# Gates of the last sixteen expert steps applied before the activations are stored

## The chip, the cores and the metric

The kernel runs on one core of a Trainium2 chip. The metric is the time of one execution on the device, in microseconds (us); lower is better. It is compared as the median of several executions. One execution is also recorded by the hardware profiler; its rows are used below.

## What is computed

One decoder layer for 544 tokens (512 of a prompt, 32 being sampled). An input projection feeds block-sparse attention and a convolution module, an output projection adds their results to the residual, and then comes the part that this change touches, a mixer of 128 x 128 = 16384 single-neuron experts, of which each of eight heads picks sixteen per token:

```python
idx = jnp.take_along_axis(cidx, pos, axis=-1)
g = jax.nn.softmax(top, axis=-1).astype(xc.dtype)
act = jax.nn.gelu(jnp.einsum('nd,nhkd->nhk', xc, expert_u[idx]), approximate=False)
return jnp.einsum('nhk,nhkd->nd', g * act, expert_v[idx])
```

## The kernel before

The kernel doesn't gather experts for most tokens. It computes all 16384 activations for all tokens as a dense product (the **up phase**), multiplies them with a matrix of gates that is zero where an expert wasn't picked, and multiplies the result with all of V (the **down phase**). Only the first 128 tokens (P) get their down product by gathered rows; the other 416 (ND) go through the dense one.

Both phases have 64 steps of 256 experts. To keep float32 accuracy on TensorE, each operand is split in a rounded part and a rest (`_hi`, `_lo`), and each product is three matmuls (lines 1394 to 1396).

**Up step s.** SP loads 1 MB of u into one of two buffers w_raw. ScalarE rounds it to w_hi (high_u, line 798), GpSimd makes w_lo (line 552), TensorE does 96 matmuls of 272 columns in two halves j. Behind each half ScalarE writes GELU to act_out (line 816), and SP stores act_out to the scratch tensor acts in HBM (line 411). SP's order within a step: wait for w_lo of step s + 1, load u of step s + 2, wait for both GELUs of step s, store them.

**Gates.** During steps 32 to 44 the matrix of gates is made and stored in HBM. It is loaded back by quads of four steps: 1664 KB for each of 16 quads into one of two halves of g_in (load_gates, line 427).

**Down step c.** SP loads act (416 KB, columns of the 416 tokens, line 424) into one of two buffers, and V in four parts to a quad, part k into v_raw[k]: w_raw[0], w_raw[1], v_raw_2 (which lies over act_out) and v_raw_3. DVE multiplies act with the gates (gate_acts, line 1325, two products of 128x416), ScalarE rounds it to a_hi (high_a, line 871), DVE makes a_lo (low_acts, line 1333). ScalarE rounds V to w_hi (high_v, line 864) once the down step two before is done, DVE makes w_lo (split_v, line 1338). TensorE then does 48 matmuls of 416 columns, and DVE adds two blocks to the residual (line 1313). DVE also adds up the 128 gathered rows (line 1355), GpSimd fetches them and the activations that belong to them (lines 568 and 561).

Every engine works through its own list in order. DVE's list for a down step is: second block of c - 1, gate_acts(c + 4), split_v(c + 1), some rows, first block of c, low_acts(c + 4), more rows.

TensorE's step c waits for `v_lo_done` of c and, at the first part of a quad, for `a_done` of all four steps of the quad.

**Between the phases.** After step 45 SP loads the gates of quads 0 and 1 and acts of steps 0 and 1; acts 2 and 3 follow after steps 48 and 49. DVE and ScalarE prepare down steps 0 to 3 in the middle of the up phase: ScalarE calls high_a(0, k) after the steps in PREPARE_AFTER (47, 48, 50, 51). At the end of the up phase SP stores the last acts, loads V parts 3 and 2 of quad 0, then acts of steps 4 and 5, then the gates of quad 2.

Of the kernel before, what the change touches and what calls it, by code (L numbers as in the profile page):

```python
# [8 lines left out]
ALU = mybir.AluOpType  # L9
# [3 lines left out]
P = 128  # L13
# [5 lines left out]
N = SEQ + NDEC  # L19
# [28 lines left out]
STEPS = 64  # L48
GCHUNK = 32
# [8 lines left out]
AFTER_GATES = RANK_STEPS + NG  # L58
PREPARE_AFTER = tuple(AFTER_GATES + n for n in (2, 3, 5, 6))
SCORE_BANKS = (4, 5, 6, 7)  # L60
# [34 lines left out]
def build_layer(nc, io):  # L95
# [95 lines left out]
    act_out = sb("act_out", [P, 2, 2, N])  # L191
# [80 lines left out]
    acts_loaded = [sem("acts_loaded0"), sem("acts_loaded1")]  # L272
    gated, a_high = sem("gated"), sem("a_high")
    g_made, g_kept = sem("g_made"), sem("g_kept")
# [75 lines left out]
    with nc.Block() as block:  # L350

        @block.sync
        def _(sp):
# [55 lines left out]
            def store_acts(s, slot):  # L409
                sp.wait_ge(gelu_done, 2 * s + 2)  # L410
                sp.dma_start(acts[s], act_out[:, slot, :, :].rearrange("p j n -> p (j n)"))\
                    .then_inc(acts_stored[slot], 16)
# [33 lines left out]
            for half in range(2):  # L446
                load_gates(half, half)
                sp.wait_ge(acts_stored[half], 32)
                load_acts(half, half)
            for s in range(AFTER_GATES + 1, AFTER_GATES + 7):  # L450
                up_step(s, s % 2)
                if AFTER_GATES + 3 <= s <= AFTER_GATES + 4:
                    first = s - AFTER_GATES - 3
                    sp.wait_ge(a_done, 2 * first + 2)
                    load_acts(first + 2, first)
            with sp.Fori((AFTER_GATES + 7) // 2, STEPS // 2 - 1) as i:
                up_step(2 * i, 0)
                up_step(2 * i + 1, 1)
            for slot in range(2):
                sp.wait_ge(u_lo_done, STEPS - 1 + slot)  # L460
                load_v(0, slot)
                store_acts(STEPS - 2 + slot, slot)
            load_v(0, 3)
# [21 lines left out]

            with sp.Fori(0, STEPS // 8 - 2) as it:
                for k in range(8):
                    down_step(it, k)
            it = STEPS // 8 - 2
            for k in range(8):  # L490
                c = 8 * it + k
                sp.wait_ge(v_lo_done, c + 1)
                load_v(2 * it + k // 4 + 1, k % 4)
                sp.wait_ge(a_done, 2 * c + 10)
                load_acts(c + 6, k % 2)
                if k == 3:
                    sp.wait_ge(gated, 2 * c + 10)
                    load_gates(2 * it + 3, 1)
            for k in range(4):
                down_step(STEPS // 8 - 1, k, True)  # L500
            sp.wait_ge(rows_added, 1)
# [85 lines left out]
        def _(sc):  # L587
# [278 lines left out]
            def high_a(it, k):  # L866

                s, slot = 8 * it + k, k % 2
                for j in range(2):
                    sc.wait_ge(gated, 2 * s + j + 1)  # L870
                    sc.activation(a_hi[k // 4 % 2][:, 2 * (k % 4) + j, :], act[:, slot, j, :], ACT.Copy)\
                        .then_inc(a_high, 1)

            plain_step(AFTER_GATES, 1, 16 * (AFTER_GATES // 2), 16 * (AFTER_GATES // 2 + 2))
            for s in range(AFTER_GATES + 1, AFTER_GATES + 7):
                plain_step(s, s % 2, 16 * (s // 2), 16 * ((s + 1) // 2) + 16)
                if s in PREPARE_AFTER:
                    high_a(0, PREPARE_AFTER.index(s))
            with sc.Fori((AFTER_GATES + 7) // 2, STEPS // 2 - 1) as i:
                plain_step(2 * i, 0, 16 * i, 16 * i + 16)  # L880
                plain_step(2 * i + 1, 1, 16 * i, 16 * i + 32)
            plain_step(STEPS - 2, 0, 8 * STEPS - 16, 8 * STEPS)
            sc.wait_ge(up_done, 2 * STEPS - 2)
            high_v(0, 64)
            for j in range(2):
                gelu_out(STEPS - 1, 1, j, 8 * STEPS - 16)
            sc.wait_ge(up_done, 2 * STEPS)
            high_v(1, 64)
# [9 lines left out]

            with sc.Fori(0, STEPS // 8 - 1) as it:
                for k in range(8):  # L900
                    down_step(it, k)
# [7 lines left out]
        def _(v):  # L909
# [406 lines left out]
            def gate_acts(s):  # L1316

                slot = s % 2
                v.wait_ge(acts_loaded[slot], 16 * (s // 2) + 16)
                if s % 4 == 0:  # L1320
                    v.wait_ge(g_loaded[s // 4 % 2], 16 * (s // 8) + 16)
                for j in range(2):
                    tile = 2 * (s % 4) + j
                    mine = act[:, slot, j, :].rearrange("p (c t) -> p c t", t=GCHUNK)
                    v.tensor_tensor(mine, mine, g_in[:, s // 4 % 2, :, GCHUNK * tile:GCHUNK * (tile + 1)], ALU.mult)\
                        .then_inc(gated, 1)
# [33 lines left out]

            for s in range(4):
                gate_acts(s)
                low_acts(s)
            split_v(0)
# [467 lines left out]
```

## Time and profile before

| | |
|---|---|
| median of three executions | 2172.93 us (2168.53 to 2173.59) |
| profiled execution, its own time | 2174.22 us |
| its span (first to last instruction) | 2172.6 us |
| TensorE busy | 2025.2 us, 93% |
| DVE busy | 1371.3 us, 63% |
| DMA, mean over the span | 193 GB/s |

The up phase ends and the down phase begins near 1571 us. A stretch in which TensorE is busy all the time can't get shorter by what other engines do; what counts there are the holes before its matmuls, which the timeline shows in square brackets, with what ended them. Times in the rows are in us from the start of the span.

### The profile page before, as it was taken

The numbers are of one execution on the slowest core, as the hardware profiler recorded it, in microseconds if no ns is written. First come the engines' busy times: TensorE is split into PE (matmuls) and PEld (weight loads), VectorE is DVE, ScalarE is ACT, GpSimd is POOL, SyncE is SP. The second block draws the span as 40 slices with busy tenths as digits, with TensorE's granted clock in tenths as the row PEclk, the third lists the DMA queues.
The fourth block names the chain that finished last, engine by engine and source line by source line (L and its number), as shares of the span: only waits on it lengthen the run. The fifth ranks groups of instructions, "written<-read, shape, count | busy, mean of one in ns | idle before, by whom it ended". The sixth has DMA issues, their size and how long they took to land.

```text
span 2172.6 us, 39130 instructions
## 1 busy us (share of the span) xinstructions
PE 2025.2 (93%) x14822; PEld 1911.2 (88%) x14822; DVE 1371.3 (63%) x2452; ACT 729.7 (34%) x940; POOL 769.9 (35%) x493
## 2 busy tenths in 40 slices
PE   6878899768999999998899999999989999999999
PEld 6877667228999999998899999999989999999999
DVE  3869673301334457999888884200068988889885
ACT  3233565202222222322355554232222332333331
POOL 3222211323233333343321222333344555655550
PEclk9998999759999999999999999999999999999999
DMA  4252655971222333333244545533589999999993
GB/s 158 63 85 101 205 198 185 359 296 60 76 78 100 123 125 129 137 132 111 98 177 165 205 180 208 195 137 129 182 289 313 332 345 307 334 326 345 323 312 108
DMA packets 202168, 420.05 MB, mean 193 GB/s; under 512 B 28129, under 2 KB 137762, under 8 KB 189250
## 3 DMA queue, kind: packets, MB, share of 16 engines
q1 hardware_dynamic: 162866, 314.92, 42.1%
q0 software_dynamic: 32768, 100.75, 13.1%
q10 hardware_dynamic: 6416, 2.78, 1.0%
q8 instruction: 77, 1.26, 0.2%
q14 instruction: 41, 0.34, 0.1%
HBM read 350.46 MB, written 67.92 MB: 193 GB/s over the span
## 4 chain that ended last, share of the span: by engine, by line
PE 45%; issue 32%; DVE 9%; POOL 6%; DMA 3%; ACT 2%; DVEq 1%; SPq 1%; POOLq 1%; ACTq 0%
PE pair L1394 13%; PE pair L1396 12%; PE pair L1395 12%; POOL w_lo L552 6%; DVE conv L972 3%; PE pair L1539 2%; DVE pair L1355 1%; DVE w_lo L1338 1%; PE pair L1551 1%; DMA v_ring<-in_cache_v 1%; DMA picked_a<-acts,at_unit 1%; DMA page_ring<-in_cache_k 1%; PE pair L1504 1%; PE pair L1526 1%; DVEq L965 1%
## 5 line engine op out<-in xcount | busy, mean ns | idle before, releaser
L1394 PE MATMUL pair<-x_hi,w_hi 128*128 128x272 f32 x2560 | 757.4, 296 | 24.1 <-DVE x_lo L928 16.2
L1396 PE MATMUL pair<-x_hi,w_lo 128*128 128x272 f32 x2560 | 744.5, 291 | 0.0
L1395 PE MATMUL pair<-x_lo,w_hi 128*128 128x272 f32 x2560 | 741.0, 289 | 0.0
L552 POOL TENSOR_TENSOR w_lo<-w_raw,w_hi 128x2048 fp32r<-128x2048 f32 x64 | 301.3, 4707 | 621.7 <-ACT w_hi L798 621.7
L1394 PEld LDWEIGHTS pair<-x_hi,w_hi 128*128 128x128 f32 x2560 | 486.9, 190 | 27.7 <-issue 22.3
L1395 PEld LDWEIGHTS pair<-x_lo,w_hi 128*128 128x128 f32 x2560 | 487.1, 190 | 0.2
L1396 PEld LDWEIGHTS pair<-x_hi,w_lo 128*128 128x128 f32 x2560 | 485.7, 190 | 0.0
L1394 PE MATMUL pair<-a_hi,w_hi 128*128 128x416 f32 x1024 | 360.7, 352 | 13.1 <-DVE w_lo L1338 7.6
L1396 PE MATMUL pair<-a_hi,w_lo 128*128 128x416 f32 x1024 | 360.9, 352 | 0.0
L1395 PE MATMUL pair<-a_lo,w_hi 128*128 128x416 f32 x1024 | 358.2, 350 | 0.0
L816 ACT ACTIVATE act_out<-pair 128x544 f32<-128x544 f32 x128 | 81.3, 635 | 462.0 <-PE pair L1396 462.0
L1394 PEld LDWEIGHTS pair<-a_hi,w_hi 128*128 128x128 f32 x1024 | 192.5, 188 | 17.2 <-issue 8.4
L568 POOL DMA_INDIRECT v_rows<-in_v_t,at_row x128 | 122.1, 954 | 229.3 <-DVE pair L1355 209.0
L1395 PEld LDWEIGHTS pair<-a_lo,w_hi 128*128 128x128 f32 x1024 | 192.8, 188 | 2.7
L1396 PEld LDWEIGHTS pair<-a_hi,w_lo 128*128 128x128 f32 x1024 | 192.4, 188 | 1.6
L561 POOL DMA_INDIRECT picked_a<-acts,at_unit x128 | 172.6, 1348 | 54.1 <-issue 38.7
L541 POOL TENSOR_TENSOR w_lo<-w_raw,w_hi 128x2048 fp32r<-128x2048 f32 x22 | 101.1, 4595 | 251.3 <-ACT w_hi L608 251.3
L1355 DVE SCALAR_TENSOR_TENSOR pair<-v_rows,share,pair 128x1024 f32<-128x1024 f32 x127 | 163.7, 1289 | 11.5
L1338 DVE TENSOR_TENSOR w_lo<-w_raw,w_hi 128x2048 fp32r<-128x2048 f32 x32 | 73.2, 2289 | 139.8 <-ACT w_hi L864 139.8
L834 ACT ACTIVATE g_out<-pair 128x512 f32<-128x512 f32 x104 | 117.1, 1126 | 122.8 <-PE pair L1716 122.8
L1716 PE MATMUL pair<-hot,hot 128*128 128x128 f32 x832 | 112.5, 279 | 16.5 <-DVE hot L1300 16.5
L798 ACT ACTIVATE w_hi<-w_raw 128x2048 fp32r<-128x2048 f32 x64 | 122.1, 1907 | 8.1 <-DMA w_raw<-in_u_t 8.0
(199 smaller groups left out, 2644.4 us busy)
## 6 DMA issues: line engine op xcount, KB each, us to landing
w_raw<-in_u_t SPq DMA_DIRECT2D x64, 1024.0 KB, 5.8
acts<-act_out SPq DMA_DIRECT2D x64, 544.0 KB, 3.0
w_raw<-in_v_t SPq DMA_DIRECT2D x128, 256.0 KB
v_raw<-in_v_t SPq DMA_DIRECT2D x128, 256.0 KB, 5.9
gates<-g_out SPq DMA_DIRECT2D x13, 2048.0 KB, 8.0
g_in<-gates SPq DMA_DIRECT2D x16, 1664.0 KB, 13.3
act<-acts SPq DMA_DIRECT2D x64, 416.0 KB, 5.9
page_ring<-in_cache_k SPq DMA_DIRECT2D x64, 256.0 KB, 2.9
```

The lines of the kernel that those rows point to most:

```text
L541: pool.tensor_tensor(w_lo[:, chunk % 2, :], w_raw[:, chunk % 2, :], w_hi[:, chunk % 2, :].bitcast(F32), ALU.subtract).then_inc(w_split, 1)
L552: pool.tensor_tensor(w_lo[:, slot, :], w_raw[:, slot, :], w_hi[:, slot, :].bitcast(F32), ALU.subtract).then_inc(u_lo_done, 1)
L561: pool.indirect_dma_start(picked_a[:, k:k + 1], None, every_unit[:, :], bass.IndirectOffsetOnAxis(ap=at_unit[:, k:k + 1], axis=0))\
L568: pool.indirect_dma_start(v_rows[:, k % RING, :], None, every_row[:, :], bass.IndirectOffsetOnAxis(ap=at_row[:, k:k + 1], axis=0))\
L798: sc.activation(w_hi[:, slot, :], w_raw[:, slot, :], ACT.Copy).then_inc(u_hi_done, 1)
L834: sc.activation(g_out[:, parity, :, TOK * q:TOK * q + TOK].rearrange("p i t -> p t i"), bank(TURN + q % 2).rearrange("p (t i) -> p t i", t ...
L1338: v.tensor_tensor(w_lo[:, c % 2, :], v_raw[c % 4], w_hi[:, c % 2, :].bitcast(F32), ALU.subtract).then_inc(v_lo_done, 1)
L1355: v.scalar_tensor_tensor(total, row, share[:, k:k + 1], total, ALU.mult, ALU.add).then_inc(row_used, 1)
L1394: te.matmul(out, s_hi, m_hi, start=start, stop=False)
L1395: te.matmul(out, s_hi, m_lo, start=False, stop=False)
L1396: return te.matmul(out, s_lo, m_hi, start=False, stop=stop)
L1716: last = te.matmul(bank(TURN + q % 2)[:, P * t:P * (t + 1)], hot1[:, q // 2 % 2, TOK * (q % 2) + t, :], hot2[:, q // 2 % 2, TOK * (q % 2) ...
```

## The change

Activations of steps 48 to 63 (GATED_UP = 48) are multiplied with their gates in the up phase, in act_out, before SP stores them; only the columns of the 416 tokens are multiplied. In the down phase these steps need no gates any more, and ScalarE's high_a waits for the load itself. So the gates of quads 12 and 13 are loaded first, those of 14, 15, 0 and 1 after steps 51, 55, 59 and 63, and the down phase loads quads 2 to 11 only. The preparation of down steps 0 to 3 moves to the last three up steps, and acts of steps 2 and 3 are loaded after the store of step 62. Some loops on SP and ScalarE are written out. The short description of the change also names four raw buffers for V; the kernel before has them already, and the diff doesn't touch v_raw.

```diff
+GATED_UP = 48
+EARLY_QUADS = (STEPS - GATED_UP) // 4
...
             def store_acts(s, slot):
-                sp.wait_ge(gelu_done, 2 * s + 2)
+                if isinstance(s, int) and s >= GATED_UP:
+                    sp.wait_ge(gated_up, 2 * (s - GATED_UP) + 2)
+                else:
+                    sp.wait_ge(gelu_done, 2 * s + 2)
...
             for half in range(2):
-                load_gates(half, half)
+                load_gates(GATED_UP // 4 + half, half)
                 sp.wait_ge(acts_stored[half], 32)
                 load_acts(half, half)
-            for s in range(AFTER_GATES + 1, AFTER_GATES + 7):
-                up_step(s, s % 2)
-                if AFTER_GATES + 3 <= s <= AFTER_GATES + 4:
-                    first = s - AFTER_GATES - 3
-                    sp.wait_ge(a_done, 2 * first + 2)
-                    load_acts(first + 2, first)
...
+            for s in range(AFTER_GATES + 1, STEPS):
+                sp.wait_ge(u_lo_done, s + 1)
+                if s + 2 < STEPS:
+                    load_u(s + 2, s % 2)
+                else:
+                    load_v(0, s % 2)
+                store_acts(s, s % 2)
+                if s >= GATED_UP and s % 4 == 3:
+                    load_gates((s // 4 + 2) % (STEPS // 4), s // 4 % 2)
+                if s == STEPS - 2:
+                    for slot in range(2):
+                        sp.wait_ge(a_done, 2 * slot + 2)
+                        load_acts(2 + slot, slot)
             load_v(0, 3)
...
+                if c % 4 == 3 and c // 4 + 3 < GATED_UP // 4:
                     sp.wait_ge(gated, 2 * c + 10)
+                    load_gates(c // 4 + 3, (c // 4 + 1) % 2)
...
                 for j in range(2):
-                    sc.wait_ge(gated, 2 * s + j + 1)
+                    if isinstance(s, int) and s >= GATED_UP:
+                        sc.wait_ge(acts_loaded[slot], 16 * (s // 2) + 16)
+                    else:
+                        sc.wait_ge(gated, 2 * s + j + 1)
...
+            high_a(0, 0)
             plain_step(STEPS - 2, 0, 8 * STEPS - 16, 8 * STEPS)
+            high_a(0, 1)
             sc.wait_ge(up_done, 2 * STEPS - 2)
             high_v(0, 64)
+            high_a(0, 2)
             for j in range(2):
                 gelu_out(STEPS - 1, 1, j, 8 * STEPS - 16)
+            high_a(0, 3)
             sc.wait_ge(up_done, 2 * STEPS)
             high_v(1, 64)
...
             def gate_acts(s):
                 slot = s % 2
+                if s >= GATED_UP:
+                    return
...
-            for s in range(4):
-                gate_acts(s)
-                low_acts(s)
+            def gate_up(s):
+                slot, quad = s % 2, s // 4
+                if s % 4 == 0:
+                    v.wait_ge(g_loaded[quad % 2], 16 * ((s - GATED_UP) // 8) + 16)
+                for j in range(2):
+                    v.wait_ge(gelu_done, 2 * s + j + 1)
+                    tile = 2 * (s % 4) + j
+                    mine = act_out[:, slot, j, P:N].rearrange("p (c t) -> p c t", t=GCHUNK)
+                    v.tensor_tensor(mine, mine, g_in[:, quad % 2, :, GCHUNK * tile:GCHUNK * (tile + 1)], ALU.mult)\
+                        .then_inc(gated_up, 1)
+
+            for s in range(GATED_UP, STEPS):
+                gate_up(s)
+                for early in {STEPS - 3: (0,), STEPS - 2: (1, 2), STEPS - 1: (3,)}.get(s, ()):
+                    gate_acts(early)
+                    low_acts(early)
             split_v(0)
```

## Rows read from the trace of the kernel before

**Rows 1.** Page, busy time of TensorE, share and instructions

```profile
PE 2025.2 (93%) x14822; PEld 1911.2 (88%) x14822; DVE 1371.3 (63%) x2452; ACT 729.7 (34%) x940; POOL 769.9 (35%) x493
```

**Rows 2.** Stretches: length, busy PE, PEld, DVE, ACT, POOL; clock, DMA share, GB/s

```profile
1390.00:1547.00 157.00, 157.00 (x1247) 157.00 (x1246) 8.21 (x10) 41.99 (x45) 59.92 (x13) 1.00 0.39 138
1572.00:1580.00 8.00, 8.00 (x44) 7.91 (x43) 0.00 (x0) 1.25 (x1) 3.74 (x4) 1.00 0.88 268
1580.00:1590.00 10.00, 3.62 (x13) 3.16 (x12) 6.13 (x9) 3.15 (x4) 6.46 (x6) 0.66 1.08 376
1349.00:1369.00 20.00, 20.00 (x161) 20.00 (x160) 1.09 (x2) 3.11 (x4) 4.60 (x1) 1.00 1.00 353
1605.00:1948.00 343.00, 338.64 (x1790) 333.86 (x1789) 298.89 (x348) 106.86 (x112) 185.49 (x158) 1.00 0.97 325
1948.00:2093.00 145.00, 144.90 (x767) 142.94 (x765) 127.99 (x149) 45.32 (x48) 75.92 (x68) 1.00 0.98 333
```

**Rows 3.** TensorE's waits from 1200 us on; timeline of four matmuls behind holes

```profile
PE pair L1394 <- DVE w_lo L1338: 7.6, 3, 6.4
...
PE pair L1394 <- DVE a_lo L1333: 3.2, 3, 1.5
...
1375.53 0.59 PE L1394 MATMUL pair<-x_hi,w_hi 128*128 128x272 f32 x1 [3.26 <-POOL w_lo L552]
1571.49 0.46 PE L1394 MATMUL pair<-a_hi,w_hi 128*128 128x416 f32 x1 [0.71 <-ACT act_out L816]
1587.22 0.72 PE L1394 MATMUL pair<-a_hi,w_hi 128*128 128x416 f32 x1 [6.38 <-DVE w_lo L1338]
...
2094.65 0.43 PE L1394 MATMUL pair<-a_hi,w_hi 128*128 128x416 f32 x1 [1.57 <-issue]
```

**Rows 4.** Timeline of SP's queue: start us, length of issue, line, transfer

```profile
1358.72 1.00 SPq L400 DMA_DIRECT2D w_raw<-in_u_t  x1
...
1523.18 0.35 SPq L411 DMA_DIRECT2D acts<-act_out  x1
1524.18 0.34 SPq L400 DMA_DIRECT2D w_raw<-in_u_t  x1
...
1577.26 1.30 SPq L424 DMA_DIRECT2D act<-acts  x2
```

**Rows 5.** Timeline of DVE

```profile
1373.40 7.32 DVE L1333 TENSOR_TENSOR a_lo<-act,a_hi 128x416 fp32r<-128x416 f32 x2 [12.36 <-ACT a_hi L871]
...
1583.87 1.09 DVE L1325 TENSOR_TENSOR act<-act,g_in 128x416 f32<-128x416 f32 x2 [20.40 <-DMA act<-acts]
1584.88 2.28 DVE L1338 TENSOR_TENSOR w_lo<-w_raw,w_hi 128x2048 fp32r<-128x2048 f32 x1
...
1587.58 1.09 DVE L1333 TENSOR_TENSOR a_lo<-act,a_hi 128x416 fp32r<-128x416 f32 x2
```

**Rows 6.** Timeline of ScalarE and of GpSimd (POOL)

```profile
1535.02 1.91 ACT L798 ACTIVATE w_hi<-w_raw 128x2048 fp32r<-128x2048 f32 x1
...
1546.61 0.63 ACT L816 ACTIVATE act_out<-pair 128x544 f32<-128x544 f32 x1 [5.43 <-PE pair L1396]
1547.13 1.91 ACT L798 ACTIVATE w_hi<-w_raw 128x2048 fp32r<-128x2048 f32 x1
...
1570.82 0.62 ACT L816 ACTIVATE act_out<-pair 128x544 f32<-128x544 f32 x1 [5.43 <-PE pair L1396]
...
1549.12 4.61 POOL L552 TENSOR_TENSOR w_lo<-w_raw,w_hi 128x2048 fp32r<-128x2048 f32 x1 [7.50 <-ACT w_hi L798]
```

**Rows 7.** DMA issues from 1345 to 1400 us: transfer, count, median us to landing

```profile
g_in<-gates SPq DMA_DIRECT2D x2, 1664.0 KB, 9.7
```

**Rows 8.** Stretches around the dips of the clock, columns as in rows 2

```profile
1374.00:1378.00 4.00, 2.47 (x11) 2.48 (x12) 4.00 (x2) 1.60 (x1) 3.72 (x2) 0.63 0.65 213
...
1583.00:1584.00 1.00, 0.00 (x0) 0.00 (x0) 0.13 (x1) 0.00 (x0) 0.79 (x1) 0.61 1.07 371
...
1590.00:1591.00 1.00, 1.00 (x7) 0.99 (x6) 1.00 (x2) 0.76 (x2) 0.00 (x0) 0.97 1.13 342
```

More of the change, by code:

```diff
@@ L58 @@
 AFTER_GATES = RANK_STEPS + NG
-PREPARE_AFTER = tuple(AFTER_GATES + n for n in (2, 3, 5, 6))
+GATED_UP = 48
+EARLY_QUADS = (STEPS - GATED_UP) // 4
 SCORE_BANKS = (4, 5, 6, 7)
@@ L272, in build_layer @@
     acts_loaded = [sem("acts_loaded0"), sem("acts_loaded1")]
-    gated, a_high = sem("gated"), sem("a_high")
+    gated, a_high, gated_up = sem("gated"), sem("a_high"), sem("gated_up")
     g_made, g_kept = sem("g_made"), sem("g_kept")
@@ L446, in _ @@
             for half in range(2):
-                load_gates(half, half)
+                load_gates(GATED_UP // 4 + half, half)
                 sp.wait_ge(acts_stored[half], 32)
                 load_acts(half, half)
-            for s in range(AFTER_GATES + 1, AFTER_GATES + 7):
-                up_step(s, s % 2)
-                if AFTER_GATES + 3 <= s <= AFTER_GATES + 4:
-                    first = s - AFTER_GATES - 3
-                    sp.wait_ge(a_done, 2 * first + 2)
-                    load_acts(first + 2, first)
[L456 to L462, printed above, removed]
+            for s in range(AFTER_GATES + 1, STEPS):
[11 more added lines that the diff above has]
+                        load_acts(2 + slot, slot)
             load_v(0, 3)
@@ L484, in down_step @@
                     load_gates(2 * it + k // 4 + 3, (k // 4 + 1) % 2)
-            with sp.Fori(0, STEPS // 8 - 2) as it:
+            first = GATED_UP // 8 - 2
+            with sp.Fori(0, first) as it:
                 for k in range(8):
                     down_step(it, k)
[L489 to L496, printed above, removed]
+            for c in range(8 * first, STEPS):
+                it, k = c // 8, c % 8
+                if c < STEPS - 4:
+                    sp.wait_ge(v_lo_done, c + 1)
+                    load_v(2 * it + k // 4 + 1, k % 4)
+                if c < STEPS - 6:
+                    sp.wait_ge(a_done, 2 * c + 10)
+                    load_acts(c + 6, c % 2)
+                if c % 4 == 3 and c // 4 + 3 < GATED_UP // 4:
                     sp.wait_ge(gated, 2 * c + 10)
-                    load_gates(2 * it + 3, 1)
-            for k in range(4):
-                down_step(STEPS // 8 - 1, k, True)
+                    load_gates(c // 4 + 3, (c // 4 + 1) % 2)
             sp.wait_ge(rows_added, 1)
@@ L874, in _ @@
             plain_step(AFTER_GATES, 1, 16 * (AFTER_GATES // 2), 16 * (AFTER_GATES // 2 + 2))
[L875 to L879, printed above, removed]
+            with sc.Fori((AFTER_GATES + 1) // 2, STEPS // 2 - 1) as i:
                 plain_step(2 * i, 0, 16 * i, 16 * i + 16)
                 plain_step(2 * i + 1, 1, 16 * i, 16 * i + 32)
+            high_a(0, 0)
             plain_step(STEPS - 2, 0, 8 * STEPS - 16, 8 * STEPS)
+            high_a(0, 1)
             sc.wait_ge(up_done, 2 * STEPS - 2)
             high_v(0, 64)
+            high_a(0, 2)
             for j in range(2):
                 gelu_out(STEPS - 1, 1, j, 8 * STEPS - 16)
+            high_a(0, 3)
             sc.wait_ge(up_done, 2 * STEPS)
@@ L897, in down_step @@
                     high_v((k + 2) % 4, 128 * it + 64 * ((k + 2) // 4) + 64)
-            with sc.Fori(0, STEPS // 8 - 1) as it:
+            with sc.Fori(0, GATED_UP // 8 - 1) as it:
+                for k in range(8):
+                    down_step(it, k)
+            for it in range(GATED_UP // 8 - 1, STEPS // 8 - 1):
                 for k in range(8):
@@ L1318, in gate_acts @@
                 slot = s % 2
+                if s >= GATED_UP:
+                    return
                 v.wait_ge(acts_loaded[slot], 16 * (s // 2) + 16)
                 if s % 4 == 0:
-                    v.wait_ge(g_loaded[s // 4 % 2], 16 * (s // 8) + 16)
+                    v.wait_ge(g_loaded[s // 4 % 2], 16 * (s // 8 + EARLY_QUADS // 2) + 16)
                 for j in range(2):
```

## Prediction

> **What bounds the kernel now.** I read the stretches first. TensorE is busy for 2025.2 of 2172.6 us [rows 1]. From 1390 to 1547 us (up phase, steps 49 to 61) it is busy all the time while the DMA engines are 39% busy; in the two long down stretches it is busy 338.64 of 343.00 and 144.90 of 145.00 us, and there the DMA engines are 97 to 98% busy, DVE 87 to 88% [rows 2]. Both phases are therefore bound by TensorE, the down phase with DMA and DVE close behind. So only the holes in TensorE's work can shrink, and only new holes can cost.
>
> The holes come next [rows 3]. There is one of 3.26 us at 1375.53 (step 48 waits for w_lo, late because u was late behind the first gate loads), 0.71 us at 1571.49 (first down step), 6.38 us at 1587.22 (second down step), then two short waits for w_lo (7.6 - 6.38 = 1.2 us), three for a_lo (3.2 us), and 1.57 us at 2094.65 with no releaser. After 6.38 the rest of the down phase holds only 6.0 us of holes (1.2 + 3.2 + 1.6), and after 1948 us, where quads 12 to 15 begin to be loaded, only the 1.57 us one. That one sits where the tensor program leaves its loop for the last two quads, and the tensor program isn't edited.
>
> Last, why the second down step is late, in the rows of SP, DVE and ACT. DVE is in order and puts gate_acts(4) ahead of split_v(1). Gate_acts(4) waits for act step 4, which SP issues at 1577.26, after the last store, eight pieces of V, and which has landed when DVE starts at 1583.87; the product (1.09) and the split follow, and TensorE starts at 1587.22, 3.35 us after the landing [rows 4, 5]. V itself and w_hi are there long before.
>
> **The change, part by part.**
>
> *Raw buffers.* v_raw has four entries before and after; the diff changes none. Nothing.
>
> *Up phase, steps 48 to 63.* DVE gets 32 products of 128x416, 0.55 us each (1.09 for two) [rows 5], 17.6 us in all, in a phase where it is busy 8.21 of 157 us [rows 2]. They run beside matmuls. Each store waits for the product behind its GELU, so SP's store, and what it queues behind it, is 0.6 us later; the act_out buffer is needed two steps on, so that is covered.
>
> *Gate loads at steps 51, 55 and 59.* They stand on SP's queue ahead of the next u. Before, the store of step 59 goes out at 1523.18, u at 1524.18 [rows 4]; that is the u of step 62, which ScalarE rounds at 1535.02 [rows 6]. With the gates in front, 0.54 + 1.70 + 1.05 = 3.3 MB must pass. At the 353 GB/s of the stretch with the first gate loads [rows 2] this is 9.3 us plus some 2 to land: 1535 to 1536. Behind the rounding GpSimd's split takes 4.61 us; for step 63 it starts at 1549.12 and ends at 1553.73, and TensorE needs it 12.1 us after the GELU at 1546.61 begins, at 1558.7 (the steps stand 12.1 us apart). So a rounding may start 5.0 us late at no cost [rows 6]. I take zero. The bounds are 0 and, for three loads each missing by 3.26 us as at 1375.53 [rows 3], 10 us.
>
> The first pair of gate loads (quads 12 and 13 now) stands where quads 0 and 1 stood, with two acts loads, and the u load stands behind them as it did, issued at 1358.72 only [rows 4]. The 3.26 us hole stays.
>
> *ScalarE's high_a(0, 0) ahead of high_u(63).* It now waits for the gate product of step 61 (0.55), the first of gate_acts(0) (0.55), and takes about 1.0: some 2.3 us ahead of the rounding that started at 1547.13. Slack is 5.0 us [rows 6]. Zero; if gates of quad 0 (issued near 1524.6) took longer than 23 us, every us more would show.
>
> *First down step.* Before, w_hi and w_lo of V chunk 0 and all of a_lo for quad 0 were ready when step 63's GELU ended, 1570.82 + 0.62 [rows 6]. Now DVE does, after that GELU and in this order: its product (0.55), gate_acts(3) (1.09), low_acts(3) (1.09, with ScalarE's high_a between, overlapping), split_v(0) (2.29) [rows 5]. Sum 5.0, handovers 0.1. TensorE starts down at 1576.5 instead of 1571.49, after 5.8 us of idling instead of 0.71. The step then runs 9.35 us (1571.49 to 1580.84 before), to 1585.9 or later.
>
> *Second down step.* Quad 1's gates (1664 KB) used to be loaded near 1351; now they are issued behind the last store, in front of V parts 3 and 2 and of act step 4. Those are 1.70 MB on DMA engines that are 88% busy from 1572 to 1580 and saturated, at 376 GB/s, from 1580 to 1590 [rows 2]. Service of 1.70 MB at 376 GB/s is 4.5 us, less 0.12 x 8 = 1.0 us of free time in the first stretch, plus about 0.8 for the later store (0.6) and the issue (0.45, in part hidden): act step 4 lands +4.3 us later, at 1588.2. Then the same 3.35 us: TensorE starts the second down step at 1591.5 rather than 1587.22. The first hole is hidden under this one: without it TensorE would only wait longer here. Bounds: from below, the end of the first down step, 1585.9 (-1.3); from above, the gates take as long alone as the pair at 1349 did per load, 9.7 us [rows 7]. I take +4.3, by the rate.
>
> In sentences apart: the Trainium skill, page "DMA: Bandwidth & Descriptors", section on queues, rings and completion order, says that the descriptors of one queue are consumed in ring order on each DMA engine. By that rule act step 4 can't overtake the gates and the whole 4.5 us counts; were it to share the engines evenly with them, it would be near nothing and the time unchanged. The trace agrees with the order: the u issued at 1358.72 was late behind the gates and acts issued before it [rows 3, 4].
>
> *Clock.* After the idling at 1580.8 TensorE was granted its lower level from within 1583 (0.61) until 1590 (0.97 in the next microsecond) [rows 8], so it ran the first 2.8 us after 1587.22 at 1.2 instead of 2.4 GHz, a cost of 1.4 us. The same should happen at 1591.5. The new idling near 1571 may add a dip inside the first down step, hidden under the wait; if the two dips together leave more of the restart slow, up to 1.7 us. I take +0.3.
>
> *Down phase.* Four gate loads of 1.70 MB go, 32 products go from DVE (17.6 us), and ScalarE's a_hi no longer waits for them. All of it after about 1948 us, where DVE has 17 us of room in 145 and TensorE is idle for 0.1 [rows 2]. Gain 0; bound -1.6, if the hole of 1.57 us were such a wait. Quads 2 to 11 keep their loads, and so the 4.4 us of holes in between. The loops unrolled on SP and ScalarE cost at most a late fetch, and ScalarE's rounding of V is hidden by some 4.9 us (a step of 9.06, as 767 matmuls at 48 to a step make 16 steps of 145 us [rows 2], less 1.9 for the rounding and 2.28 for the split [rows 5, 6]).
>
> *Sum.* +4.3 + 0.3 + 0 = +4.6 us against a span of 2172.6 and an own time of 2174.22 (2178.8); the profiled run stood 1.3 us above the median of 2172.93, so the median becomes 2177.5, +0.21%. Less than 0.3% (6.5 us) is about what a measurement of this kernel can't tell from no change.
>
> **Rivals.**
> 1. *The gates are hidden in the queue.* The first wait is swallowed and act step 4 lands within 2 us of before: 2171.6 to 2175. For it: 1.0 us of free DMA time and a queue that is nearly empty at 1572. Against: saturation from 1580 on [rows 2].
> 2. *The up phase gets holes.* A gate load makes u late, or DVE's products hold GpSimd's split. Rows: the hole at 1375.53, and a_lo which took 7.32 us for two instead of 1.09 beside two splits [rows 5]. Each hole would be 3.3 us [rows 3] plus some 1.5 of slow clock (0.63 granted from 1374 to 1378 [rows 8]); one or two on top of +4.6 give 2182 to 2187. It decides once u lands over 5.0 us late. Against: one load instead of two with two acts. Apart from this: the Trainium skill, page "SBUF — State Buffer", section on who interferes with whom, says that a VectorE instruction with two SBUF inputs and a GpSimd one that reads SBUF exclude each other, the first holding the pair for its whole length; by it DVE's 0.55 us can shift a split by as much, ten times less than the slack, so its cost would be 0, and a 4.6 us delay of a product is covered too.
> 3. *Faster, by the down phase.* Relief of DMA and DVE in the last 16 steps closes holes, and the emptier queue brings picked_a in earlier. The price is at most all holes there, 6.0 us, plus the second down step at its lower bound, -1.3: 2172.93 - 7.3 = 2165.6. It decides only if the second step doesn't lose and nearly all holes go, of which all but 1.57 us lie ahead of the relieved stretch. A model in which DMA, not TensorE, sets the pace would give it: 6.8 MB less at 330 GB/s are 20 us. Against: TensorE busy 144.90 of 145.00.
>
> **Chances.** Forecast (+2 to +6.5, and its tail to +9) 0.55, of which 0.10 is above 6.5 us; rival 1 0.13; rival 2 0.22; rival 3 0.10. Faster 0.10, same 0.45 + 0.13 = 0.58, slower 0.10 + 0.22 = 0.32. Range: down to rival 1's low end and a little under, 2171, up through the forecast's tail and half of rival 2, 2184.
>
> **What would show it.** Right: a TensorE hole of 5 to 6 us ahead of the first down step, released by w_lo; a second of 5 to 7 us, ended 3.35 us after act step 4 lands near 1588; no new hole between 1390 and 1571; DVE near 76% busy after 1990, with TensorE as before. Wrong: act step 4 landing by 1585 (rival 1), u late at steps 54, 58 or 62 (rival 2), or a down phase shorter than 64 x 9.06 plus its holes. The prediction fails most easily on the 1.70 MB: on how far the DMA engines take them beside V.

## The result and the profile after

The changed kernel takes 2181.51 us (2177.73 to 2184.93, five executions), the kernel before, on the same chip, 2172.17 us. The ratio is 1.0043 with a 95% interval of 1.0028 to 1.0057, some 6 to 12 us: slower, by a little more than the 0.3% that a measurement here can tell. A second series gave 1.0040 (1.0022 to 1.0058). The forecast was +4.6 us (2177.5, range 2171 to 2184), so its sign and place were right and the time lies in its range, but its size was half of the measured one, and "within 0.3%", its likeliest case, did not happen.

The profiled execution of the changed kernel took 2177.73 us, the fastest of its five, with a span of 2176.1 us.

The holes of TensorE in the timeline, all of them from 1340 us on (in brackets the idle time and what ended it):

```profile
1373.56 0.38 PE L1420 MATMUL pair<-x_hi,w_hi 128*128 128x272 f32 x1 [3.27 <-POOL w_lo L556]
1575.99 0.69 PE L1420 MATMUL pair<-a_hi,w_hi 128*128 128x416 f32 x1 [6.95 <-DVE w_lo L1350]
1592.62 0.72 PE L1420 MATMUL pair<-a_hi,w_hi 128*128 128x416 f32 x1 [5.58 <-DVE w_lo L1350]
1685.60 0.45 PE L1420 MATMUL pair<-a_hi,w_hi 128*128 128x416 f32 x1 [0.29 <-DVE w_lo L1350]
1696.43 0.45 PE L1420 MATMUL pair<-a_hi,w_hi 128*128 128x416 f32 x1 [1.48 <-DVE a_lo L1345]
...
1823.62 0.45 PE L1420 MATMUL pair<-a_hi,w_hi 128*128 128x416 f32 x1 [0.29 <-DVE w_lo L1350]
1842.39 0.45 PE L1420 MATMUL pair<-a_hi,w_hi 128*128 128x416 f32 x1 [0.37 <-DVE a_lo L1345]
1879.78 0.46 PE L1420 MATMUL pair<-a_hi,w_hi 128*128 128x416 f32 x1 [0.84 <-DVE a_lo L1345]
2025.79 0.45 PE L1420 MATMUL pair<-a_hi,w_hi 128*128 128x416 f32 x1 [0.67 <-DVE a_lo L1345]
```

Beside [rows 3] the reader sees three things: the hole at step 48 is the same, the 0.71 us ahead of the first down step has become 6.95, and the 1.57 us near 2094 is gone.

Absolute times mislead here. The stretch before 1340 us, which the change doesn't touch, ended at different times in different executions. The last matmul of the up phase stood at 1570.8 us before and at 1569.0 after, and between 1566 and 1578 in nine of the profiles of the experiments (earlier only in the two without the hole at step 48). So I measure from that last matmul (the first down matmul's start less its hole). To the second down step it is 16.4 us before (1570.8 to 1587.2) and 23.6 after (1569.0 to 1592.6): +7.1. From there to the end of the span it is 585.4 before and 583.5 after: -1.9. Together +5.2; in a second profile of the changed kernel 608.3 - 601.8 = +6.5. The first is just under the interval of its series (+6 to +12 us), the second at the low end of it.

The stretch ahead of that matmul adds little. From the last matmuls that make the gates, in the part that the change doesn't touch, to the last matmul of the up phase it is 235.9 us before, 236.1 and 236.8 in the two profiles of the changed kernel. Their places, in this order, are:

```profile
1334.90 1.05 PE L1716 MATMUL pair<-hot,hot 128*128 128x128 f32 x8
```

```profile
1332.92 1.05 PE L1742 MATMUL pair<-hot,hot 128*128 128x128 f32 x8
1330.13 1.05 PE L1742 MATMUL pair<-hot,hot 128*128 128x128 f32 x8
```

SP's queue between the phases, beside [rows 4]:

```profile
1558.25 0.35 SPq L415 DMA_DIRECT2D acts<-act_out  x1
1558.64 2.38 SPq L428 DMA_DIRECT2D act<-acts  x2
1561.07 3.65 SPq L407 DMA_DIRECT2D w_raw<-in_v_t  x4
1571.35 0.34 SPq L415 DMA_DIRECT2D acts<-act_out  x1
1571.73 0.43 SPq L431 DMA_DIRECT2D g_in<-gates  x1
1572.21 9.01 SPq L407 DMA_DIRECT2D v_raw<-in_v_t  x8
1581.27 1.49 SPq L428 DMA_DIRECT2D act<-acts  x2
```

And DVE there, beside [rows 5]:

```profile
1568.00 1.09 DVE L1337 TENSOR_TENSOR act<-act,g_in 128x416 f32<-128x416 f32 x2 [7.54 <-DMA act<-acts]
1569.21 1.09 DVE L1345 TENSOR_TENSOR a_lo<-act,a_hi 128x416 fp32r<-128x416 f32 x2
1570.22 1.11 DVE L1382 TENSOR_TENSOR act_out<-act_out,g_in 128x416 f32<-128x416 f32 x2
1571.24 1.09 DVE L1337 TENSOR_TENSOR act<-act,g_in 128x416 f32<-128x416 f32 x2
1572.44 1.09 DVE L1345 TENSOR_TENSOR a_lo<-act,a_hi 128x416 fp32r<-128x416 f32 x2
1573.45 2.29 DVE L1350 TENSOR_TENSOR w_lo<-w_raw,w_hi 128x2048 fp32r<-128x2048 f32 x1
1589.27 1.09 DVE L1337 TENSOR_TENSOR act<-act,g_in 128x416 f32<-128x416 f32 x2 [13.53 <-DMA act<-acts]
1590.28 2.28 DVE L1350 TENSOR_TENSOR w_lo<-w_raw,w_hi 128x2048 fp32r<-128x2048 f32 x1
```

The chain is the forecast one: the gates of quad 1 stand behind the last store; V's eight pieces take 9.01 us to issue; act step 4 is issued at 1581.27 and has landed when DVE starts at 1589.27; TensorE follows 3.35 us later, to the hundredth as before. From last store to landing it is 17.9 us, 12.4 before. Most of the difference is already there when act step 4 is issued: 9.9 us after the last store, 5.8 before (1577.26 less 1571.47), where SP issued the eight pieces in 5.36 us:

```profile
1571.47 0.35 SPq L411 DMA_DIRECT2D acts<-act_out  x1
1571.86 5.36 SPq L406 DMA_DIRECT2D v_raw<-in_v_t  x8
```

What I hadn't seen is the first line of DVE: act step 2, issued at 1558.64, lands only at 1568.00. DVE and ScalarE wait for it, the last products and the last store come 1.0 us late behind it, and the store stands 2.3 us behind the last matmul, 0.7 before.

The stretches beside [rows 2] and [rows 8] (columns as there):

```profile
1390.00:1547.00 157.00, 157.00 (x1247) 157.00 (x1246) 26.37 (x28) 38.61 (x39) 59.87 (x13) 1.00 0.49 165
1572.00:1580.00 8.00, 4.01 (x12) 3.87 (x13) 3.62 (x4) 2.71 (x3) 3.54 (x4) 0.57 0.98 293
1580.00:1590.00 10.00, 7.03 (x38) 6.62 (x36) 0.73 (x2) 0.11 (x1) 5.03 (x6) 1.00 1.08 350
1948.00:2093.00 145.00, 144.33 (x765) 142.62 (x764) 116.42 (x128) 45.20 (x48) 74.64 (x69) 1.00 0.86 283
...
1592.00:1594.00 2.00, 1.38 (x4) 1.33 (x5) 2.00 (x5) 0.74 (x1) 0.00 (x0) 0.50 1.09 385
1594.00:1596.00 2.00, 2.00 (x8) 1.90 (x7) 2.00 (x5) 0.90 (x2) 0.00 (x0) 0.50 0.87 276
1596.00:1598.00 2.00, 2.00 (x10) 1.96 (x9) 1.77 (x1) 0.15 (x1) 0.00 (x0) 0.79 0.84 289
```

The up phase hides all 26 us of DVE and the extra gate loads. From 1948 to 2093 us DVE falls from 88 to 80% and the DMA engines from 98 to 86% busy, and TensorE's 145 us stay nearly as full as they were (144.33 us busy, 144.90 before). There are two dips of the clock now, one inside the first down step (which runs 11.05 us instead of 9.35, hidden) and one that holds the second at 1.2 GHz until about 1597.

### The profile page after: what moved, and what is told of

Read it like the earlier page. It is cut to its first block, busy times and chain, and to the rows that moved or that the text cites. A ratio compares the mean times of both kernels' runs of the same rounds, so it can differ in the third digit from the quotient of the medians.

```text
span 2176.1 us, 38846 instructions
## 1 busy us (share of the span) xinstructions
PE 2022.5 (93%) x14822; PEld 1911.4 (88%) x14822; DVE 1378.5 (63%) x2452; ACT 729.8 (34%) x940; POOL 764.6 (35%) x493
## 4 chain that ended last, share of the span: by engine, by line
PE 43%; issue 31%; DVE 10%; POOL 6%; DMA 5%; ACT 2%; DVEq 1%; SPq 1%; POOLq 0%; ACTq 0%
PE pair L1420 12%; PE pair L1422 12%; PE pair L1421 12%; POOL w_lo L556 6%; DVE conv L982 3%; PE pair L1565 2%; DMA v_ring<-in_cache_v 1%; DMA page_ring<-in_cache_k 1%; DVE pair L1367 1%; DVE w_lo L1350 1%; DMA picked_a<-acts,at_unit 1%; PE pair L1577 1%; DMA act<-acts 1%; PE pair L1530 1%; DVEq L975 1%
## 5 line engine op out<-in xcount | busy, mean ns | idle before, releaser
L565 POOL DMA_INDIRECT picked_a<-acts,at_unit x128 | 167.3, 1307 | 53.5 <-issue 38.7
L1382 DVE TENSOR_TENSOR act_out<-act_out,g_in 128x416 f32<-128x416 f32 x32 | 31.4, 985 | 196.6 <-ACT act_out L820 196.6
```

Source lines behind the costliest of these rows:

```text
L565: pool.indirect_dma_start(picked_a[:, k:k + 1], None, every_unit[:, :], bass.IndirectOffsetOnAxis(ap=at_unit[:, k:k + 1], axis=0))\
```

## The experiments

In the table, "to 2nd" is the time from the last matmul of the up phase to the start of the second down step, "to end" from there to the end of the span; "sum" is both, each from one profile. A ratio is of times, to the kernel before, measured beside it. "No hole" means that TensorE doesn't wait before the second down step.

| kernel | ratio (95%) | to 2nd | to end | sum |
|---|---|---|---|---|
| before | 1 | 16.4 | 585.4 | 601.8 |
| changed | 1.0043 (1.0028 to 1.0057) | 23.6 | 583.5 | 607.1 |
| changed, again | 1.0040 (1.0022 to 1.0058) | 24.0 | 584.3 | 608.3 |
| before, gates of quad 1 again | 1.0029 (1.0010 to 1.0047) | 22.1 | 588.0 | 610.1 |
| before, preparation late | 0.9983 (0.9968 to 0.9997) | 17.4 | 584.3 | 601.7 |
| before, acts early | 0.9956 (0.9940 to 0.9973) | 9.9, no hole | 584.4 | 594.3 |
| changed, acts first | 0.9995 (0.9980 to 1.0011) | 17.9, no hole | 583.0 | 600.9 |
| changed, split first | 1.0018 (1.0001 to 1.0034) | 24.2 | 585.9 | 610.0 |
| changed, acts and split first | 0.9991 (0.9975 to 1.0007) | 18.0 | 584.2 | 602.2 |
| changed, act step 2 early | 1.0012 (0.9998 to 1.0025) | 22.5 | 582.9 | 605.4 |
| changed, four gate loads more | 1.0027 (1.0010 to 1.0044) | 23.3 | 584.2 | 607.5 |
| before, loads spread | 0.9942 (0.9917 to 0.9967) | 9.9, no hole | 583.9 | 593.8 |
| the same, gates of quad 2 early | 0.9928 (0.9910 to 0.9946) | 9.9, no hole | 583.6 | 593.5 |

**The changed kernel again.** No edit.

> The changed kernel once more, for a second profile and its time beside the others. Queue theory (act step 4 waits in SP's queue behind the gates of quad 1, and that alone sets the second down step): the same two holes of 5.5 to 7 us before the first two down steps, no new hole elsewhere, time 2178 to 2185 us, ratio to before near 1.004. Rival (the loss of the median lies in the up phase, of which the first profile happened to show none): this profile shows a hole in steps 49 to 63, or a longer stretch before 1340 us.

Measured: 2182.47 us beside 2173.77; holes of 7.31 and 6.14 us before the first two down steps, none in steps 49 to 63, and the stretch before 1340 us isn't longer (the rows above). The rival of a loss in the up phase falls for this profile; its execution (2176.82 us) was one at the low end of the series (2176.78 to 2186.71).

**Before, with the gates of quad 1 loaded again behind the last store.**

```diff
+            load_gates(1, 1)
             load_v(0, 3)
...
-                    v.wait_ge(g_loaded[s // 4 % 2], 16 * (s // 8) + 16)
+                    v.wait_ge(g_loaded[s // 4 % 2], 16 * (s // 8 + s // 4 % 2) + 16)
```

> The kernel before, with nothing changed but that the gates of quad 1 are loaded a second time into the same half of g_in, behind the last store and ahead of V part 3, as the changed kernel loads them; gate_acts(4) waits for this second load. The DVE chain ahead of the first down step stays short. Queue theory: the second down step starts 4.5 to 6 us later than before, the hole there grows from 6.4 to 11 or 12 us, time +5 to +7 us (2177 to 2179.5). Rival (it is the work of DVE between the phases, or the gating itself, that costs): within 1.5 us of before.

Measured: 2182.2 us; the hole before the second down step is 12.0 us and it starts 22.1 us after the up phase, +5.6. This one load, with no gating and no moved preparation, makes most of the later start of the second down step. (Its profile also has +2.6 us behind that start. 0.7 of it is a longer second step; the rest lies in several small holes later in the down phase, which no run explains.) The DMA engines beside it, first this kernel and then the kernel before, 8 us from the last store on and then up to the landing of act step 4:

```profile
1566.99:1574.99 8.00, 7.97 (x42) 7.89 (x43) 0.00 (x0) 1.77 (x1) 2.87 (x4) 1.00 0.90 263
1574.99:1585.01 10.02, 1.38 (x8) 1.02 (x6) 0.00 (x0) 0.00 (x0) 5.64 (x6) 0.70 1.07 343
```

```profile
1571.47:1579.47 8.00, 7.97 (x42) 7.90 (x43) 0.00 (x0) 1.77 (x1) 3.21 (x4) 1.00 0.83 254
1579.47:1583.87 4.40, 1.37 (x8) 1.02 (x6) 0.00 (x0) 0.00 (x0) 3.40 (x4) 0.93 1.02 352
```

In the first 8 us only (263 - 254) x 8 = 0.07 MB more pass. Over the whole wait the rows give 5.54 MB here and 3.58 MB before: 1.96 MB more, the gates' 1.70 and some 0.26 MB of other packets, whose loads the rows don't name. The 1.89 MB behind the first 8 us take 5.5 us at 343 GB/s.

**Before, with only the preparation moved to the end of the up phase.** No step is gated early.

```diff
-                if AFTER_GATES + 3 <= s <= AFTER_GATES + 4:
-                    first = s - AFTER_GATES - 3
-                    sp.wait_ge(a_done, 2 * first + 2)
-                    load_acts(first + 2, first)
...
                 store_acts(STEPS - 2 + slot, slot)
+                for x in range(2) if slot == 0 else ():
+                    sp.wait_ge(a_done, 2 * x + 2)
+                    load_acts(2 + x, x)
...
+            high_a(0, 0)
             plain_step(STEPS - 2, 0, 8 * STEPS - 16, 8 * STEPS)
+            high_a(0, 1)
```

(and high_a(0, 2) and high_a(0, 3) around the last GELUs, as in the change)

> The kernel before with one part of the change: down steps 0 to 3 are prepared at the end of the up phase (ScalarE's order and the loads of act steps 2 and 3 as in the changed kernel), no step is gated early and the gates are loaded as before. If the queue and the late last store make the whole loss: a first hole of 4 to 5 us, the second down step only 1.0 us later than before (17.4 us after the last matmul of the up phase instead of 16.4), time +1 to +2 us. If moving the preparation costs by itself: second down step at 20 us or more, time +4 us and more.

Measured: a first hole of 5.20 us (expected 4 to 5) and the second down step 17.4 us after the up phase, as expected to the tenth; sum 601.7, time 2171.65 us, not slower, where +1 to +2 us was expected. A hole of 5.2 us ahead of the first down step is free as long as act step 4 sets the second. It is barely so here: the hole and its dip of the clock take up the wait but for 0.28 us, and the second down step then takes 9.2 us instead of 10.5, its clock no longer low.

**Changed, act step 2 loaded 9 us earlier.**

```diff
+                if s == STEPS - 2:
+                    sp.wait_ge(a_done, 2)
+                    load_acts(2, 0)
                 store_acts(s, s % 2)
...
                 if s == STEPS - 2:
-                    for slot in range(2):
-                        sp.wait_ge(a_done, 2 * slot + 2)
-                        load_acts(2 + slot, slot)
+                    sp.wait_ge(a_done, 4)
+                    load_acts(3, 1)
```

> The changed kernel, but act step 2 is loaded right behind V part 0, 9 us earlier, ahead of the store of step 62. In the profiles of the changed kernel it lands 9.4 us after its issue and low_acts(2) then holds DVE past the last GELU, so that the last store goes out 2.3 us after the last matmul of the up phase, 0.7 in the kernel before; 0.6 of the 1.6 us is the gate product. If the late act step 2 is the other 1.0: the last store 1.3 to 1.5 us after the last matmul, the second down step 22.6 to 23.0 us after it instead of 23.6 to 24.0, time 1 us less. If the order of ScalarE or the queue alone matters: 23.6 to 24.0 again.

Measured: the last store 1.3 us after the last matmul (2.3 in the changed kernel), the second down step 22.5 us after it, sum 605.4. So 1.0 us of the loss was act step 2. The time, 2178.37 us, points the same way: the interval of its ratio (to 1.0025) ends below that of the first series of the changed kernel (from 1.0028), but reaches into that of the second (from 1.0022).

**Changed, V chunk 0 split early.**

```diff
                     low_acts(early)
+                    if early == 1:
+                        split_v(0)
-            split_v(0)
```

> The changed kernel, but DVE splits V chunk 0 right behind low_acts(1), in the wait of step 62, and not at the end of its list between the phases. Hidden-hole theory (the first hole costs nothing, since act step 4 sets the second down step): the first hole shrinks from 6.95 to some 4.5 us, the second grows by as much plus what the clock gave, the second down step starts 23.5 us after the last matmul of the up phase as before, time as the changed kernel within 2 us. Rival (the two dips of the clock belong to the two holes, and a shorter first hole saves one): 2 to 3 us less.

Measured: the first hole shrinks to 4.56, the second grows to 8.24 us, and the second down step stands at 24.2 us (expected 23.5; 23.6 and 24.0 in the changed kernel): hidden, as forecast. The time, 2179.57 us with a ratio of 1.0018, is a little lower than the changed kernel's; the intervals overlap.

```profile
1577.13 0.68 PE L1421 MATMUL pair<-a_hi,w_hi 128*128 128x416 f32 x1 [4.56 <-DVE a_lo L1345]
1596.73 0.71 PE L1421 MATMUL pair<-a_hi,w_hi 128*128 128x416 f32 x1 [8.24 <-DVE w_lo L1350]
```

**Changed, acts of steps 4 and 5 ahead of V parts 3 and 2.**

```diff
+            for slot in range(2):
+                sp.wait_ge(a_done, 2 * slot + 6)
+                load_acts(4 + slot, slot)
             load_v(0, 3)
...
             load_v(0, 2)
-            for slot in range(2):
-                sp.wait_ge(a_done, 2 * slot + 6)
-                load_acts(4 + slot, slot)
```

> The changed kernel, but acts of steps 4 and 5 are issued behind the last store and the gates of quad 1, ahead of V parts 3 and 2. Queue theory: 2 MB less stand in front of act step 4, it lands near 1582 to 1584 instead of 1589.3, the second hole shrinks to 0 to 1 us, the first (6.95) stays; 5 to 6 us less than the changed kernel, 2175 to 2177. Rival (the chain of DVE, or the slow clock behind the first hole, sets the second step): no gain, 2180 to 2183.

Measured: the second hole is gone, the first (7.38 us) stays, sum 600.9; 2173.61 us beside 2173.77 before, 1 to 3 us less than expected. The changed kernel is as fast as the kernel before once two loads of 416 KB overtake V. That doesn't make the change free: the kernel before gains too when its acts are loaded early (below, there still earlier), and beside that one (594.3) the sum here is 6.6 us longer. With the second hole gone, the first is no longer hidden. DVE, with act step 4 landed at 1585.67:

```profile
1576.55 2.28 DVE L1350 TENSOR_TENSOR w_lo<-w_raw,w_hi 128x2048 fp32r<-128x2048 f32 x1
1585.67 1.09 DVE L1337 TENSOR_TENSOR act<-act,g_in 128x416 f32<-128x416 f32 x2 [6.83 <-DMA act<-acts]
1586.68 2.29 DVE L1350 TENSOR_TENSOR w_lo<-w_raw,w_hi 128x2048 fp32r<-128x2048 f32 x1
```

**Both edits.**

> The changed kernel with both edits: acts of steps 4 and 5 ahead of V parts 3 and 2, and V chunk 0 split early. With the second hole gone the first one is in the open: it should now count in full, so 2.3 us less than with the acts alone (2173.6), near 2171 us, and 1 us more if its dip of the clock gets shorter. If the first hole were still hidden: 2173.6 again.

Measured: 2173.9 us, no gain over the acts alone. The first hole shrank by 2.4 to 5.00 us and a second of 1.87 came back, so only 0.5 us was won of the holes, and the sum of this profile, 602.2, is no lower than 600.9. DVE starts on act step 4 at 1584.65, 12.0 us after the last store, though V no longer stands ahead of it: what it waits for is then the gates of quad 1, or act step 4 right behind them; the rows don't tell which. With the first step begun earlier, that was the next thing late. Against the expectation, the first hole did not count in full in the profile; the times can't tell 2171 from 2173.9 us (the ratio reaches from 0.9975 to 1.0007).

**Before, acts of steps 4 and 5 loaded after step 51.**

```diff
+            for slot in range(2):
+                sp.wait_ge(a_done, 2 * slot + 6)
+                load_acts(4 + slot, slot)
             with sp.Fori((AFTER_GATES + 7) // 2, STEPS // 2 - 1) as i:
```

(taken out behind load_v(0, 2))

> The kernel before, but acts of steps 4 and 5 are loaded right after the store of step 51, as soon as their buffers are free, not behind eight pieces of V. Queue theory: the hole of 6.38 us before the second down step goes and its dip of the clock with it, 1.4 us: 2164 to 2166 us. Rival (behind act step 4 something else is as late, V part 1 or its split): 2170 us or more.

Measured: no hole before the second down step and no dip after it, sum 594.3 (-7.5), 2166.07 us. The 6.38 us of the kernel before were the place of two loads in a queue.

**Changed, with the gates of quads 12 to 15 loaded in the down phase as well.** Nothing reads them.

```diff
+                elif c % 4 == 3 and c // 4 + 3 < STEPS // 4:
+                    sp.wait_ge(gated, min(2 * c + 10, 2 * GATED_UP))
+                    sp.wait_ge(g_loaded[(c // 4 + 1) % 2], 16 * (8 + (c >= 47)))
+                    load_gates(c // 4 + 3, (c // 4 + 1) % 2)
```

> The changed kernel, but the gates of quads 12 to 15 are loaded in the down phase too, at the places where the kernel before loads them; nothing reads them. DVE keeps its relief of 32 products, the DMA engines lose theirs. Up to the second down step nothing changes. If the 1.9 us that the changed kernel takes less from the second down step to the end come from the DMA engines, that stretch grows from 583.5 to 585.5 us and the hole where the tensor program leaves its loop (1.6 to 2.4 us in three kernels with these loads, 0 to 0.4 in three without) comes back; if they come from DVE, it stays at 583.5 to 584.3. Time 2181 to 2185 or 2179 to 2183 us: too close to tell by the time, the stretch and the hole decide.

Measured: 584.2 us from the second down step to the end, between the two profiles of the changed kernel, and no hole near 2095, with the four loads back. So it isn't the relief of the DMA engines that closes this hole. That it is DVE's, the timeline of DVE in the kernel before shows, where its hole [rows 3] stood:

```profile
2086.45 0.17 DVE L1348 TENSOR_TENSOR share<-share,picked_a 128x8 f32<-128x8 f32 x1 [2.96 <-DMA picked_a<-acts,at_unit]
...
2088.39 1.09 DVE L1325 TENSOR_TENSOR act<-act,g_in 128x416 f32<-128x416 f32 x2
2089.39 2.29 DVE L1338 TENSOR_TENSOR w_lo<-w_raw,w_hi 128x2048 fp32r<-128x2048 f32 x1
...
2093.47 1.09 DVE L1333 TENSOR_TENSOR a_lo<-act,a_hi 128x416 fp32r<-128x416 f32 x2
2094.64 1.29 DVE L1355 SCALAR_TENSOR_TENSOR pair<-v_rows,share,pair 128x1024 f32<-128x1024 f32 x1
```

DVE loses 2.96 us waiting for gathered activations, and low_acts of step 59 ends at 2094.56; TensorE, which needs a_done of the whole quad, starts at 2094.65. The row calls the releaser "issue", but it is this a_lo. ScalarE isn't late: its a_hi, which this a_lo reads, was done at 2090.07:

```profile
2089.01 1.06 ACT L871 ACTIVATE a_hi<-act 128x416 fp32r<-128x416 f32 x2 [2.95 <-DVE act L1325]
```

In the changed kernel DVE goes from the same wait to the same a_lo without the gate products, in 7.1 us (2091.02 to 2098.11) instead of 8.1 (2086.45 to 2094.56):

```profile
2091.02 0.17 DVE L1360 TENSOR_TENSOR share<-share,picked_a 128x8 f32<-128x8 f32 x1 [2.01 <-DMA picked_a<-acts,at_unit]
...
2097.03 1.08 DVE L1345 TENSOR_TENSOR a_lo<-act,a_hi 128x416 fp32r<-128x416 f32 x2
```

Without the gate products (1.09) in the list, the hole is 0 to 0.4 us in the seven profiles of kernels that gate early; in the six of kernels that don't it is 1.3 to 2.4 us.

**Before, acts early and the first gate loads spread.**

```diff
             for half in range(2):
-                load_gates(half, half)
                 sp.wait_ge(acts_stored[half], 32)
-                load_acts(half, half)
             for s in range(AFTER_GATES + 1, AFTER_GATES + 7):
-                up_step(s, s % 2)
+                sp.wait_ge(u_lo_done, s + 1)
+                load_u(s + 2, s % 2)
+                if s < AFTER_GATES + 3:
+                    load_gates(s - AFTER_GATES - 1, s - AFTER_GATES - 1)
+                    load_acts(s - AFTER_GATES - 1, s - AFTER_GATES - 1)
+                store_acts(s, s % 2)
```

> The kernel before with acts of steps 4 and 5 early and, in addition, the first two pairs of gates and acts loads each behind the u load of their step (46 and 47), not both ahead of the u of step 48. This tests what the hole of 3.3 us at step 48 is: if u is late behind 4.2 MB of gates and acts on SP's queue, the hole and its dip go, 4 to 5 us less than with early acts alone (2166.1): 2161 to 2162.5 us. If something else holds u, no change.

Measured: the hole at step 48 is gone from the profile, so it was the place of u in the queue; 2164.55 us, 1.5 less than with early acts alone, within what the two intervals leave open. The 4 to 5 us that were expected of it are not shown by the time.

**And the gates of quad 2 in the up phase.** load_gates(2, 0) moves behind the early acts.

> The kernel before with acts of steps 4 and 5 early, the first gate loads spread over two steps, and the gates of quad 2 loaded in the up phase too. 1.7 MB less stand on the queue between the phases. If that stretch is now bound by TensorE: no hole up to quad 2 and the same time as with the spread loads, 2160 to 2165 us, under both kernels. If the DMA queue still delays V or acts there: 1 us less.

Measured: 2159.85 us, ratio 0.9928 (0.9910 to 0.9946): the lowest median here, ahead of both kernels. The sum from the up phase on is 593.5, as with the spread loads (593.8), and the intervals of the two overlap: that the gates of quad 2 add anything isn't shown.

## Why the prediction was half right

*The bound, and the two holes.* Right. TensorE bounds both phases, the change adds a hole ahead of the first down step (forecast 5.8, measured 6.95 us), it is hidden, and the second down step is set by act step 4 behind the gates of quad 1, with the same 3.35 us behind the landing. Shown by four kernels, in the start of the second down step: the load alone makes +5.6 us, the moved preparation alone +0.9, an earlier split nothing, and with the acts ahead of V the second hole is gone.

*The step that was mis-sized: "act step 4 lands +4.3 us later".* It lands so that the second down step is +7.1. Two terms of it were too small. The service of 1.70 MB was put at 4.5 us less 1.0 of free DMA time; it is 5.5 to 5.6, since the free share of the first 8 us took only 0.07 MB more, the rest ran at 343 and not at 376 GB/s, and 0.26 MB more of other packets passed before act step 4 landed. And the last store was put 0.6 us late; it is 1.6 (2.0 in the second profile), because act step 2 lands 9.4 us after its issue and DVE's list holds the last products behind it. The Trainium skill, page "DMA: Bandwidth & Descriptors", section on queues, rings and completion order, says that descriptors of one queue are consumed in ring order on each DMA engine. The prediction read it as the whole 4.5 us without the refund; the load alone, at +5.6, agrees with the order and costs more than that.

*Clock.* +0.3 was forecast; the second step runs at 1.2 GHz from 1592.6 to about 1597 instead of 1587.2 to 1590. The step takes 11.1 us (1592.62 to 1603.70) instead of 10.5 (1587.22 to 1597.68), beside 9.07 for the third: +0.6. In the second profile it takes 10.6: +0.1.

*Up phase: zero.* Right. ScalarE waited 1.7, 2.2 and 2.7 us for the u behind the gates of steps 51, 55 and 59, inside the 5.0 us of slack. One gate product took 3.67 us instead of 0.59 (at 1539.47) beside GpSimd's split (1538.09, 4.59 us); the split stayed as long as before (4.61) and the store was in time. The longest wait of ScalarE:

```profile
1536.10 1.92 ACT L802 ACTIVATE w_hi<-w_raw 128x2048 fp32r<-128x2048 f32 x1 [2.71 <-DMA w_raw<-in_u_t]
```

*Down phase: zero.* The hole of 1.57 us was put down to the tensor program leaving its loop. That was wrong: it was a late a_lo, and DVE's relief closes it or leaves 0.4 us. In the two profiles of the changed kernel the stretch from the second down step on is 1.9 and 1.1 us shorter, with the longer dip of the clock in it; from the third step on it is 572.4 and 573.7 us instead of 574.9. That is more than one pair of profiles: in the seven profiles of kernels that gate early this stretch is 571.4 to 574.2 us (573.0 with the four gate loads back), in the six others 573.9 to 576.9, the means 1.9 us apart. Rival 3 named the effect; its price needed every hole of the phase, and the others stayed or moved: a hole of 0.67 us at 2025.79, for an a_lo, is new beside the first profile of the kernel before, though kernels that don't gate early have one there too.

*What stays open.* The profiles explain +7.1 and +7.6 us up to the second down step, +0.6 and +0.1 in it and -2.5 and -1.2 behind it: +5.2 and +6.5 us. The medians say +9.3 and +8.7 with lower ends of 6 and 5. The rest may be no more than the spread of single executions (7 us among the first five of the changed kernel), and both profiles of the changed kernel are of executions at the low end of their series. Between the last matmuls that make the gates and the end of the up phase they have only +0.2 and +0.9 us. Whether the longer executions lose something else, no run here settles.

## What to carry to other kernels

Where a phase begins behind a queue, order the queue by what is needed first and not by size: a 416 KB load behind 2 MB of V cost 7.5 us here, and the change put 1.7 MB more in front of it. Price a transfer that joins a filled queue by its bytes over the rate that the queue reaches at that place (1.70 MB at 343 GB/s are 5.0 us here, 5.5 to 5.6 were measured), with no refund for a busy share under 1. And look at what a fix of the queue leaves: here it took away the second hole and brought the first, which had been free, into the open. And a saving on an engine that isn't the bound is worth the holes that it leaves today, which have to be followed one by one to the instruction that ends last, as the name beside a hole can be missing.

## What the runs showed of the hardware

DMA engines that were 83% busy were no reserve for one more transfer: with 1.70 MB more queued, the first 8 us behind the last store rose from 0.83 to 0.90 busy and from 254 to 263 GB/s only. The queue held up SP too: it issued the same eight loads of V in 9.01 us in the changed kernel, in 9.40 with the load alone, in 5.36 before.

The kernel before had one dip of the clock after 1540 us, the changed kernel two, one with each of its holes of 6.95 and 5.58 us; a hole of 3.3 us at step 48 was enough for one as well (0.63 granted on average in [rows 8]). The down step behind the first hole, 9.35 us long before, took 11.05 us.

The same instructions ahead of the change took different times: eleven profiles reach the end of the up phase anywhere from 1566 to 1578 us, and the last matmuls that make the gates, ahead of any edit, start at 1334.90 us in the kernel before and at 1332.92 and 1330.13 in the changed one. A difference of a few us between two kernels can't be read from the ends of two single profiles; measured from a common event next to the change, the two profiles of the changed kernel agree to 0.5 us on the start of the second down step and to 0.8 on the stretch behind it.
